# Feed-forward gate tiles in pairs: seven half products in place of eight

## The chip, the cores and the metric

One core of one Trainium2 chip runs the whole program. The metric is the device time of one execution in microseconds (us), the median of several runs. All arithmetic is in fp32; matmuls get their operands as fp32r and the kernel makes fp32 accuracy from them by splitting (below).

## What is computed

The reference is two transformer blocks in a row on 512 tokens of width 1024, with 16 meta tokens ahead of them. Each has two attention branches, a gated mix, and a feed-forward block of width 2816. The change touches the feed-forward blocks only:

```python
hn = rms_norm(h, ffn_norm_g[l])
h = h + (jax.nn.silu(hn @ w_ffn_gate[l]) * (hn @ w_ffn_up[l])) @ w_ffn_down[l]
```

The second block has the same form with its own weights.

## The kernel before

Everything is kept transposed: a tile has 128 features on the partitions and the 512 tokens along the free axis. A product of 128 output features takes one weight tile of 1024 x 128 (eight chunks of 128 x 128, KD = 8) and the eight chunks of the activations. Each operand is split in two fp32r parts, a high part (ScalarE's copy to fp32r) and a low part (the rest, a subtraction by VectorE), and three matmuls stand for one: high x high, high x low, low x high. `product` (L1736) issues them, 24 for a tile, into psL[:, b]; b is 0 or 1 and alternates, so that one half of psL is filled while the other is read.

The weights go through three buffers of two slots each (slot b): `load` (L455, SyncE) brings a tile from HBM into stage[:, b] once the low part of the tile before it in this slot is made (lo[b]); `high` (L720, ScalarE) writes wh[:, b], after the tile has landed (w_in[b]) and TensorE is through with the old wh[:, b] (mm[b]); `low` (L1058, VectorE) writes wl[:, b] and counts lo[b]. TensorE's product waits for lo[b] and for ev[b], the reader's signal that psL[:, b] has been read for the pair before. All of this is counted by a running number of the pair (PAIR0 of the phase, plus i). There is no planner: every engine has its own program, written out by hand, and works through it strictly in order.

The feed-forward block is done in three parts a, b and c of 8, 8 and 6 hidden tiles of 128 (FPARTS, L39). A part has a phase gu, whose pair i is gate tile i (b = 0) and up tile i (b = 1), and a phase dn of four pairs of output tiles. In gu the reader is VectorE's `swiglu` (L1497): gate times R, the tokens' norm factors (L1509); ScalarE's tanh (L936); (tanh + 1) times gate (L1513); up times R (L1515); their product, hid (L1517); ScalarE's high part of hid (L940); VectorE's low part (L1519). ScalarE's side is `swiglu` at L930. In dn, VectorE adds the product to hT (`add_down`, L1531). Before the first gu phase, the out phase makes hn from hT chunk by chunk (`squares_and_gain`, L911: hn at L916, squares at L918), and the first gu pair holds the norm factors' own small matmuls.

GpSimd (POOL) has nothing to do in the feed-forward. TensorE's order there is `layer_rest` at L2028.

Of the kernel before, what the change touches and what calls it, by code (L numbers as in the profile page):

```python
# [29 lines left out]
P = 128  # L30
D = 1024
KD = D // P
SEQ = 512
NB = SEQ // P
# [17 lines left out]

NEAR = 2 * P
# [30 lines left out]
def feed_forward(l):  # L84
    return [f for ab, n in zip("abc", FPARTS) for f in ((f"gu{l}{ab}", 2 * n, KD, 1), (f"dn{l}{ab}", KD, n, 1))]

# [131 lines left out]
def build(nc, t, out):  # L218
    with ExitStack() as ctx:
# [219 lines left out]
        recip_ok, kbm_ok = sem("recip_ok"), sem("kbm_ok")  # L439
        fin_gain, fin_rms, fin_out = sem("fin_gain"), sem("fin_rms"), sem("fin_out")  # L440
# [13 lines left out]
        def _(sp):  # L454
# [38 lines left out]
            def layer_rest(l, win, gates_at, wa, wb, wo, wg, wu, wd):  # L493
# [9 lines left out]
                for part, ab in enumerate("abc"):  # L503
                    f0 = sum(FPARTS[:part])
                    with sp.Fori(0, PAIRS[f"gu{l}{ab}"]) as i:
                        load(f"gu{l}{ab}", i, 0, by_rows(wg), i * P + f0 * P)
                        load(f"gu{l}{ab}", i, 1, by_rows(wu), i * P + f0 * P)
# [206 lines left out]
        def _(act):  # L714
# [196 lines left out]
            def squares_and_gain(name, norm, grow):  # L911

                def chunk(i, b):
# [4 lines left out]
                    act.activation(sq[:], hT[:, bass.ds(2 * i + b, 1), :], ACT.Square).then_inc(h_sq, 1)  # L918

# [10 lines left out]
            def swiglu(name, f0, early=0):  # L930
                def pair(i, last, early=False):
                    high(name, i, 1)
                    if early:
                        high_next(name, i, last)
                    act.wait_ge(ev[0], PAIR0[name] + i + 1)
                    act.activation(ft[:, 1, :], ft[:, 0, :], ACT.Tanh, scale=0.5).then_inc(t_ok, 1)  # L936
                    if not early:
                        high_next(name, i, last)
                    act.wait_ge(hid_ok, f0 + i + 1)
                    act.activation(hid[:, 0, bass.ds(i, 1), :], ft[:, 4, :], ACT.Copy).then_inc(hid_hi, 1)  # L940

                for i in range(early):
                    pair(i, False, True)
                with act.Fori(early, PAIRS[name] - 1) as i:
                    pair(i, False)
                pair(PAIRS[name] - 1, True)
# [3 lines left out]
            swiglu("gu1a", before_part(1, 0), 1)  # L950
            only_high("dn1a")
            swiglu("gu1b", before_part(1, 1))
            only_high("dn1b")
            swiglu("gu1c", before_part(1, 2))
# [65 lines left out]
            swiglu("gu2a", before_part(2, 0), 1)  # L1020
            only_high("dn2a")
            swiglu("gu2b", before_part(2, 1))
            only_high("dn2b")
            swiglu("gu2c", before_part(2, 2))
# [26 lines left out]
        def _(v):  # L1051
# [445 lines left out]
            def swiglu(name, f0, head=None):  # L1497

                def pair(i, last, head=None):
                    low(name, i, 1)  # L1500
                    if head:
                        new_rms(head[0])
                        diagonals(diag, rs[:, 0:4]).then_inc(diag_ok, 1)
                        low_next(name, i, last)
                        v.wait_ge(bcast, head[1])
                        v.tensor_copy(R, psT[:, 1, :]).then_inc(R_ok, 1)
                        v.wait_ge(R_ok, head[1])
                    done(name, i, 0)
                    v.tensor_tensor(ft[:, 0, :], psL[:, 0, :], R, ALU.mult).then_inc(ev[0], 1)  # L1509
                    if not head:  # L1510
                        low_next(name, i, last)
                    v.wait_ge(t_ok, f0 + i + 1)
                    dv.link(v.scalar_tensor_tensor(out=ft[:, 2, :], in0=ft[:, 1, :], scalar=1.0, in1=ft[:, 0, :], op0=ALU.add, op1=ALU.mult))  # L1513
                    done(name, i, 1)
                    v.tensor_tensor(ft[:, 3, :], psL[:, 1, :], R, ALU.mult).then_inc(ev[1], 1)  # L1515
                    v.wait_ge(ev[1], PAIR0[name] + i + 1)
                    v.scalar_tensor_tensor(out=ft[:, 4, :], in0=ft[:, 2, :], scalar=0.5, in1=ft[:, 3, :], op0=ALU.mult, op1=ALU.mult).then_inc(hid_ok, 1)  # L1517
                    v.wait_ge(hid_hi, f0 + i + 1)
                    v.tensor_tensor(hid[:, 1, bass.ds(i, 1), :], ft[:, 4, :], hid[:, 0, bass.ds(i, 1), :].bitcast(F32), ALU.subtract).then_inc(hid_lo, 1)  # L1519

                first = 0
                if head:
                    pair(0, False, head)
                    first = 1
                with v.Fori(first, PAIRS[name] - 1) as i:
                    dv.enter(i - first, 1)
                    pair(i, False)
                dv.leave(PAIRS[name] - 1 - first)
                pair(PAIRS[name] - 1, True)
# [6 lines left out]
            def down(name):  # L1536
                def pair(i, last):
                    low(name, i, 1)
                    add_down(name, i, 0)
                    low_next(name, i, last)  # L1540
                    add_down(name, i, 1)

                pairs(name, pair)
# [3 lines left out]
            swiglu("gu1a", before_part(1, 0), (2, 3))  # L1547
            down("dn1a")
            swiglu("gu1b", before_part(1, 1))
            down("dn1b")  # L1550
            swiglu("gu1c", before_part(1, 2))

# [157 lines left out]
            swiglu("gu2a", before_part(2, 0), (4, 5))  # L1710
            down("dn2a")
            swiglu("gu2b", before_part(2, 1))
            down("dn2b")
            swiglu("gu2c", before_part(2, 2))
# [512 lines left out]
```

## Time and profile before

| | before |
|---|---|
| median of 3 runs | 1549.47 us (1549.3 to 1551.33) |
| the profiled execution's own time | 1552.76 us |
| its span, first to last instruction | 1551.00 us |
| mean granted TensorE clock | 0.995 of full |
| TensorE matmuls | 7356, busy 1521.8 us |
| VectorE busy | 845.6 us |
| ScalarE busy | 532.7 us |
| first feed-forward block, without a wait of TensorE | 411.50 to 735.06 us |

The profile shows one execution. PE is TensorE's matmuls and PEld its weight loads, which run beside them; DVE is VectorE, ACT ScalarE, POOL GpSimd, SP SyncE. Matmuls overlap in the pipeline: a row's duration is longer than the slot that it takes, and the distance between starts tells the pitch. Times in the rows are us from the start of the span unless they are marked ns; [x <-Y] behind a row is the idle time before it and what ended it.

### The profile page before, as it was taken

Reading aid. Unit: us, or ns where it says so; the run is one execution under the profiler, and the core shown is the slowest. Engines: PE = TensorE matmul, PEld = TensorE weight load, DVE = VectorE, ACT = ScalarE, POOL = GpSimd, SP = SyncE. Lnnn points to the kernel's source line nnn. Section 1 sums busy time; section 2 is a strip of 40 time slices with the busy share of each in tenths; the row PEclk is TensorE's granted clock in tenths of the full one; section 3 lists DMA queues with packets and bytes.
Section 4 is the critical chain, followed back from the end, with each engine's and each line's share of the span. In section 5 each row is a group of like instructions: output and inputs, shape, how many; then the busy total and the mean of one; then the engine's idle time right before and its main releaser. Section 6 shows DMA issues by size and latency. Waiting matters only on the chain.

```text
span 1551.0 us, 21003 instructions
## 1 busy us (share of the span) xinstructions
PE 1521.8 (98%) x7356; PEld 1236.4 (80%) x7356; DVE 845.6 (55%) x1520; ACT 532.7 (34%) x929; POOL 242.1 (16%) x206
## 2 busy tenths in 40 slices
PE   7999999999999999999999999999999999999998
PEld 6878886877788888888899777787787888888876
DVE  5578895466555355445854383544655543553454
ACT  5134445533322223222511364444332222221223
POOL 2323334340000000000002563322300000000000
PEclk9999999999999999999999999999999999999999
DMA  6524420033333333332323202121332332333322
GB/s 151 150 55 146 129 55 1 8 92 106 94 95 95 95 95 95 95 94 86 92 84 93 55 2 82 55 61 35 107 96 84 92 103 87 95 95 96 94 81 95
DMA packets 250283, 132.61 MB, mean 85 GB/s; under 512 B 21225, under 2 KB 247653, under 8 KB 250222
## 3 DMA queue, kind: packets, MB, share of 16 engines
q1 hardware_dynamic: 247998, 123.92, 28.1%
q0 software_dynamic: 2144, 7.77, 1.6%
q8 instruction: 35, 0.57, 0.2%
q14 instruction: 26, 0.21, 0.0%
q10 hardware_dynamic: 80, 0.14, 0.0%
HBM read 129.67 MB, written 6.38 MB: 88 GB/s over the span
## 4 chain that ended last, share of the span: by engine, by line
PE 91%; DVE 5%; issue 1%; DMA 1%; ACT 1%; POOL 0%; SPq 0%; DVEq 0%; ACTq 0%; POOLq 0%
PE psL L1756 62%; PE psL L1895 11%; PE psS L1756 5%; PE psT L1904 2%; PE psS L2149 1%; PE psL L2023 1%; PE psS L2172 1%; PE psS L2000 1%; PE psS L1930 1%; PE psL L2126 1%; PE psS L1943 1%; DMA xin<-in_x 1%; PE psS L2105 1%; PE psS L2106 1%; PE psS L1917 0%
## 5 line engine op out<-in xcount | busy, mean ns | idle before, releaser
L1756 PE MATMUL psL<-hn,wh 128*128 128x512 f32 x1680 | 529.0, 396 | 0.2
L1756 PEld LDWEIGHTS psL<-hn,wh 128*128 128x128 f32 x1680 | 314.1, 188 | 76.1 <-issue 1.4
L726 ACT ACTIVATE wh<-stage 128x1024 fp32r<-128x1024 f32 (+3 forms) x250 | 243.3, 973 | 336.4 <-PE psL L1756 243.5
L1756 PE MATMUL psL<-hn,wl 128*128 128x512 f32 x840 | 330.4, 393 | 0.0
L1064 DVE TENSOR_TENSOR wl<-stage,wh 128x1024 fp32r<-128x1024 f32 (+1 forms) x169 | 202.5, 1198 | 93.7 <-ACT wh L726 89.0
L1756 PE MATMUL psL<-hid,wh 128*128 128x512 f32 x704 | 221.5, 395 | 1.3 <-DVE wl L1064 1.3
L576 POOL TENSOR_TENSOR wl<-stage,wh 128x1024 fp32r<-128x1024 f32 (+2 forms) x81 | 154.6, 1909 | 307.3 <-ACT wh L726 307.3
L1756 PEld LDWEIGHTS psL<-hn,wl 128*128 128x128 f32 x840 | 158.0, 188 | 35.8
L1895 PE MATMUL psL<-hn,wh 128*128 128x512 f32 x496 | 173.0, 430 | 0.4 <-DVE yn L1670 0.4
L1756 PEld LDWEIGHTS psL<-hid,wh 128*128 128x128 f32 x704 | 131.3, 187 | 35.3 <-DVE wl L1064 3.0
L1756 PE MATMUL psL<-hid,wl 128*128 128x512 f32 x352 | 138.8, 394 | 0.0
L1895 PEld LDWEIGHTS psL<-hn,wh 128*128 128x128 f32 x496 | 88.7, 189 | 19.3 <-DVE yn L1670 0.8
L940 ACT ACTIVATE hid<-ft 128x512 f32 (+1 forms) x44 | 27.8, 632 | 209.0 <-DVE ft L1517 209.0
L1895 PE MATMUL psL<-hn,wl 128*128 128x512 f32 x248 | 97.9, 395 | 0.0
L1534 DVE TENSOR_TENSOR hT<-hT,psL 128x512 f32 (+1 forms) x48 | 33.0, 688 | 106.0 <-PE psL L1756 106.0
L1756 PE MATMUL psS<-hn,wh 128*128 128x264 f32 x448 | 85.9, 292 | 0.8 <-DVE hn L1114 0.7
L1756 PE MATMUL psL<-mix,wh 128*128 128x512 f32 x256 | 80.7, 396 | 1.0 <-DVE wl L1064 1.0
L936 ACT ACTIVATE ft<-ft 128x512 f32<-128x512 f32 x44 | 27.9, 633 | 149.1 <-DVE ft L1509 149.1
L1756 PEld LDWEIGHTS psL<-hid,wl 128*128 128x128 f32 x352 | 65.9, 187 | 16.2
L1756 PEld LDWEIGHTS psS<-hn,wh 128*128 128x128 f32 x448 | 71.9, 194 | 2.5 <-issue 1.2
L648 POOL MEMSET m8d<- 128x128 f32 x1 | 0.2, 210 | 437.2 <-DVE kaT L1191 437.2
L1756 PE MATMUL psS<-hn,wl 128*128 128x264 f32 x224 | 64.9, 290 | 0.0
(383 smaller groups left out, 1971.4 us busy)
## 6 DMA issues: line engine op xcount, KB each, us to landing
stage<-in_w_in SPq DMA_DIRECT2D x54, 512.0 KB, 3.9
stage<-in_w_ffn_gate SPq DMA_DIRECT2D x22, 512.0 KB, 3.8
stage<-in_w_ffn_up SPq DMA_DIRECT2D x22, 512.0 KB, 3.8
stage<-in_w_ff_gate SPq DMA_DIRECT2D x22, 512.0 KB, 3.8
stage<-in_w_ff_up SPq DMA_DIRECT2D x22, 512.0 KB, 3.8
stage<-in_w_out SPq DMA_DIRECT2D x16, 512.0 KB, 3.8
stage<-in_w_ffn_down SPq DMA_DIRECT2D x16, 512.0 KB, 3.8
stage<-in_w_ff_down SPq DMA_DIRECT2D x16, 512.0 KB, 3.9
```

The lines of the kernel that those rows point to most:

```text
L576: pool.tensor_tensor(wl[:, b, 0:n], stage[:, b, 0:n], wh[:, b, 0:n].bitcast(F32), ALU.subtract).then_inc(lo[b], 1)
L726: act.activation(wh[:, b, 0:n], stage[:, b, 0:n], ACT.Copy).then_inc(hi[b], 1)
L936: act.activation(ft[:, 1, :], ft[:, 0, :], ACT.Tanh, scale=0.5).then_inc(t_ok, 1)
L940: act.activation(hid[:, 0, bass.ds(i, 1), :], ft[:, 4, :], ACT.Copy).then_inc(hid_hi, 1)
L1064: v.tensor_tensor(wl[:, b, 0:n], stage[:, b, 0:n], wh[:, b, 0:n].bitcast(F32), ALU.subtract).then_inc(lo[b], 1)
L1534: v.tensor_tensor(hT[:, n, :], hT[:, n, :], psL[:, b, :], ALU.add).then_inc(ev[b], 1)
L1756: ins = pe.matmul(dst, w[:, b, k * P:(k + 1) * P], x[:, part, k, c0:c1], start=k + n == 0, stop=k == kc - 1 and n == 2)
L1895: ins = pe.matmul(psL[:, b, :], w[:, b, k * P:(k + 1) * P], hn[:, part_, k, META:], start=k + n == 0, stop=k == KD - 1 and n == 2)
L1904: ins = pe.transpose(psT[:, n % 2, m * P:(m + 1) * P], tile[:, col:col + P], ident[:])
L1930: pe.matmul(psS[:, 2 * (j % 2), 0:W], aqT[:, h % 4, i * P:(i + 1) * P], akz[:, h // 4, k0:k0 + W], start=True, stop=True).then_inc(p["s"], 1)
L1943: ins = pe.matmul(psS[:, 2 * (i % 2) + 1, h * HD:(h + 1) * HD], PTa[:, u % 2, n * P:(n + 1) * P], avn[:, c, h // 4 * HD:h // 4 * HD + HD], ...
L2000: ins = pe.matmul(psS[:, 2 * (j % 2) + bank, 0:k1 - k0], q, kz[:, h, k0:k1], start=True, stop=True)
```

## The change

A gate tile's product is written as a 2 x 2 block product: two gate tiles (rows i and i + 1) by the two halves of the contraction (chunks 0 to 3, 4 to 7), times two halves of the tokens (256 each). In place of eight products of blocks come seven, by Strassen's scheme in the form with shared sums; each is 4 chunks x 3 split matmuls of 256 columns. Up tiles, down tiles and the first four gate tiles of part a are made as before. For this, the change

- loads two gate tiles as one pair and then the two up tiles as the next pair;
- makes a copy hg of the activations with their gain (ScalarE, in the out phase) and, in pairs 1 to 3 of part a, four sums of token blocks from it, each 128 x 1024, with high and low parts (xt);
- makes for each gate pair four sums of weight blocks (VectorE, 128 x 512 each), with high (ScalarE) and low (VectorE) parts, two of 128 x 1024 each;
- takes interim results out of PSUM by ScalarE (part_x, part_z) and adds them on VectorE.

```diff
+GATE_PLAIN = (4, 0, 0)
...
 # SyncE, layer_rest
+                    for i in range(GATE_PLAIN[part]):
+                        load(f"gu{l}{ab}", i, 0, by_rows(wg), (f0 + i) * P)
+                        load(f"gu{l}{ab}", i, 1, by_rows(wu), (f0 + i) * P)
+                    for i, _ in gate_pairs(l, part):
+                        for b in range(2):
+                            load(f"gu{l}{ab}", i, b, by_rows(wg), (f0 + i + b) * P)
+                        for b in range(2):
+                            load(f"gu{l}{ab}", i + 1, b, by_rows(wu), (f0 + i + b) * P)
...
 # ScalarE, squares_and_gain
+                    act.activation(hg[:, bass.ds(2 * i + b, 1), :], hT[:, bass.ds(2 * i + b, 1), :], ACT.Copy,
+                                   scale=gvec[:, bass.ds(2 * i + (grow + b), 1)]).then_inc(hg_ok, 1)
 # ScalarE
+            def sum_high(pair, half):
+                act.wait_ge(ws_sum, 2 * pair + half + 1)
...
+                act.activation(wsh[:, cols], wsum[:, cols], ACT.Copy).then_inc(ws_hi, 1)
+            def second_high(name, i):
+                act.wait_ge(w_in[1], 16 * (LOAD0[name] + LOADS[name]) + i * (16 * LOADS[name]))
+                act.wait_ge(mm[1], PAIR0[name] + i)
+                act.activation(wh[:, 1, SEQ:2 * SEQ], stage[:, 1, SEQ:2 * SEQ], ACT.Copy).then_inc(hi[1], 1)
...
+            def swiglu(l, part):
...
+                for i in range(plain):
                     high(name, i, 1)
+                    if i == 0:
+                        high_next(name, i, False)
                     act.wait_ge(ev[0], PAIR0[name] + i + 1)
                     act.activation(ft[:, 1, :], ft[:, 0, :], ACT.Tanh, scale=0.5).then_inc(t_ok, 1)
+                    if i:
+                        high_next(name, i, False)
+                    if i == 1:
+                        token_sum_high(l, 0)
+                        token_sum_high(l, 1)
+                        inner_high(i, f0)
+                        token_sum_high(l, 2)
+                    elif i == 2:
+                        token_sum_high(l, 3)
+                        inner_high(i, f0)
+                    elif i == plain - 1:
+                        sum_high(pairs_[0][1], 0)
+                        inner_high(i, f0)
+                        sum_high(pairs_[0][1], 1)
...
+                second_high(name, pairs_[0][0])
+                for i, n in pairs_:
+                    last = i == pairs_[-1][0]
+                    act.wait_ge(acc_x, 3 * n + 1)
+                    act.activation(part_x[:, 0:HT], psS[:, 0, 0:HT], ACT.Copy).then_inc(out_x, 1)
+                    high(name, i + 1, 0)
+                    act.wait_ge(mm[1], PAIR0[name] + i + 1)
+                    act.activation(part_z[:, 0:HT], psS[:, 3, 0:HT], ACT.Copy).then_inc(out_z, 1)
+                    high(name, i + 1, 1)
+                    act.wait_ge(acc_y, 2 * n + 1)
+                    act.activation(part_z[:, HT:], psS[:, 2, 0:HT], ACT.Copy).then_inc(out_y, 1)
+                    act.wait_ge(acc_x, 3 * n + 2)
+                    act.activation(part_x[:, HT:], psS[:, 0, 0:HT], ACT.Copy).then_inc(out_x, 1)
...
+                    if not last:
+                        sum_high(n + 1, 0)
+                    high_next(name, i + 1, last)
+                    inner_high(i, f0)
+                    if not last:
+                        sum_high(n + 1, 1)
+                        second_high(name, i + 2)
+                    inner_high(i + 1, f0)
...
 # VectorE, swiglu: the plain pairs of part a
                     done(name, i, 0)
                     v.tensor_tensor(ft[:, 0, :], psL[:, 0, :], R, ALU.mult).then_inc(ev[0], 1)
+                    if i == first - 1:
+                        weight_sums(name, first, pair0)
+                    if i:
+                        low_next(name, i, False)
+                    opened(i, f0, ft[:, 0, :], ft[:, 1, :])
+                    if i == 1:
+                        token_sum(l, 0)
+                        token_sum(l, 1)
+                        token_sum_low(l, 0)
+                        token_sum(l, 2)
+                    elif i == 2:
+                        token_sum_low(l, 1)
+                        token_sum(l, 3)
+                        token_sum_low(l, 2)
+                    elif i == first - 1:
+                        sum_low(pair0, 0)
+                    times_up(name, i, 1, i, f0, ft[:, 0, :])
+                    if i == first - 1:
+                        second_low(name, first)
+                    inner_low(i, f0)
+                    if i == first - 1:
+                        sum_low(pair0, 1)
 # VectorE, swiglu: a gate pair and its up pair
+                for i, n in pairs_:
+                    last = i == pairs_[-1][0]
+                    done(name, i, 0)
+                    v.wait_ge(out_x, 2 * n + 1)
+                    v.tensor_tensor(ft[:, 0, 0:HT], psS[:, 1, 0:HT], part_x[:, 0:HT], ALU.add).then_inc(ev[0], 1)
+                    low(name, i + 1, 0)
+                    low(name, i + 1, 1)
+                    v.wait_ge(acc_y, 2 * n + 2)
+                    v.wait_ge(out_x, 2 * n + 2)
+                    dv.link(v.tensor_tensor(ft[:, 0, HT:], psS[:, 2, 0:HT], part_x[:, HT:], ALU.add))
+                    v.tensor_tensor(ft[:, 0, :], ft[:, 0, :], R, ALU.mult).then_inc(gate_ok, 1)
...
+                    opened(i, f0, ft[:, 0, :], ft[:, 1, :])
+                    opened(i + 1, f0, ft[:, 2, :], tanh2[:])
+                    if not last:
+                        weight_sums(name, i + 2, n + 1)
+                    times_up(name, i, 0, i + 1, f0, ft[:, 0, :])
+                    low_next(name, i + 1, last)
+                    if not last:
+                        sum_low(n + 1, 0)
+                    inner_low(i, f0)
+                    if not last:
+                        sum_low(n + 1, 1)
+                    times_up(name, i + 1, 1, i + 1, f0, ft[:, 2, :])
+                    if not last:
+                        second_low(name, i + 2)
+                    inner_low(i + 1, f0)
...
 # TensorE
+            def half_product(dst, weights, c0, x, add=False):
+                whi, wlo = weights
+                for k in range(KD // 2):
+                    cols = slice(c0 + k * P, c0 + (k + 1) * P)
+                    for n, (w, part) in enumerate(((whi, 0), (whi, 1), (wlo, 0))):
+                        ins = pe.matmul(dst, w[:, cols], x(part, k), start=not add and k + n == 0, stop=k == KD // 2 - 1 and n == 2, skip_group_check=True)
+                return ins
+            def gate_pair(name, i, n, l):
...
+                for b in range(2):
+                    pe.wait_ge(ev[b], PAIR0[name] + i)
+                pe.wait_ge(lo[0], PAIR0[name] + i + 1)
+                half_product(x, first, 0, rows_of(0, 0)).then_inc(acc_x, 1)
+                half_product(psS[:, 1, 0:HT], first, SEQ, rows_of(KD // 2, 0)).then_inc(mm[0], 1)
+                pe.wait_ge(lo[1], PAIR0[name] + i + 1)
+                pe.wait_ge(xt_lo, 4 * l)
+                half_product(z, second, SEQ, token_sums(3)).then_inc(mm[1], 1)
+                pe.wait_ge(ws_lo, 2 * n + 1)
+                half_product(y, mixed, 0, token_sums(0)).then_inc(acc_y, 1)
+                pe.wait_ge(out_x, 2 * n + 1)
+                half_product(x, mixed, SEQ, token_sums(1), add=True).then_inc(acc_x, 1)
+                pe.wait_ge(ws_lo, 2 * n + 2)
+                pe.wait_ge(out_y, n + 1)
+                half_product(y, mixed, 2 * SEQ, rows_of(KD // 2, HT), add=True).then_inc(acc_y, 1)
+                pe.wait_ge(out_x, 2 * n + 2)
+                half_product(x, mixed, 3 * SEQ, token_sums(2), add=True).then_inc(acc_x, 1)
+                for b in range(2):
+                    product(name, i + 1, b, hn)
```

`weight_sums` waits for both of the gate pair's loads and issues four tensor_tensor of 128 x 512; `sum_low` is one subtraction of 128 x 1024 after its `sum_high`; `second_low` one of 128 x 512 after `second_high`; `token_sum` and `token_sum_low` are one of 128 x 1024 each. `times_up` is up times R, which counts ev[b], and then hid; `opened` is (tanh + 1) times gate; `inner_low` is the low part of hid. In `down` the weight sums, the sum_low and the second_low for the next part's first gate pair stand in the last pair.

## Rows read from the trace of the kernel before

**Rows 1.** The page: busy time by engine, TensorE's clock in slices, chain's shares
```profile
PE 1521.8 (98%) x7356; PEld 1236.4 (80%) x7356; DVE 845.6 (55%) x1520; ACT 532.7 (34%) x929; POOL 242.1 (16%) x206
...
PEclk9999999999999999999999999999999999999999
...
PE 91%; DVE 5%; issue 1%; DMA 1%; ACT 1%; POOL 0%; SPq 0%; DVEq 0%; ACTq 0%; POOLq 0%
PE psL L1756 62%; PE psL L1895 11%; PE psS L1756 5%; PE psT L1904 2%; PE psS L2149 1%; PE psL L2023 1%; PE psS L2172 1%; PE psS L2000 1%; PE psS L1930 1%; PE psL L2126 1%; PE psS L1943 1%; DMA xin<-in_x 1%; PE psS L2105 1%; PE psS L2106 1%; PE psS L1917 0%
```

**Rows 2.** The chain in order of time (start, us, what): the two feed-forward blocks
```profile
411.50 323.56 PE psL L1756 x1392
...
1179.52 323.57 PE psL L1756 x1392
```

**Rows 3.** Busy time of each engine in two stretches of the feed-forward
```profile
core 0: us, PE busy (x) PEld busy (x) DVE busy (x) ACT busy (x) POOL busy (x), PEclk, DMA share, GB/s
...
600.00:700.00 100.00, 100.00 (x432) 80.67 (x431) 44.09 (x51) 24.30 (x28) 0.00 (x0) 1.00 0.32 95
1210.00:1310.00 100.00, 100.00 (x432) 80.67 (x431) 44.41 (x51) 23.91 (x29) 0.00 (x0) 1.00 0.32 95
```

**Rows 4.** VectorE's timeline over one pair of part a (start, us, engine, instruction)
```profile
428.64 0.69 DVE L1509 TENSOR_TENSOR ft<-psL,Rk 128x512 f32<-128x512 f32 x1 [1.10 <-PE psL L1756]
430.98 1.22 DVE L1064 TENSOR_TENSOR wl<-stage,wh 128x1024 fp32r<-128x1024 f32 x1 [1.65 <-ACT wh L726]
432.12 0.68 DVE L1513 SCALAR_TENSOR_TENSOR ft<-ft 128x512 f32<-128x512 f32 x1
434.27 0.69 DVE L1515 TENSOR_TENSOR ft<-psL,Rk 128x512 f32<-128x512 f32 x1 [1.47 <-PE psL L1756]
...
439.76 0.69 DVE L1509 TENSOR_TENSOR ft<-psL,Rk 128x512 f32<-128x512 f32 x1 [1.11 <-PE psL L1756]
```

**Rows 5.** The chain in order of time: the stretch of matmuls with 264 columns
```profile
783.33 49.07 PE psS L1756 x405
```

**Rows 6.** VectorE's groups by form: 1024, 768 and 512 elements (busy us, mean ns)
```profile
L1064 DVE TENSOR_TENSOR wl<-stage,wh 128x1024 fp32r<-128x1024 f32 x153 | 187.3, 1224 | 85.9 <-ACT wh L726 81.2
...
L1515 DVE TENSOR_TENSOR ft<-psL,Rk 128x512 f32<-128x512 f32 x44 | 30.4, 692 | 62.8 <-PE psL L1756 62.7
...
L1064 DVE TENSOR_TENSOR wl<-stage,wh 128x768 fp32r<-128x768 f32 x16 | 15.2, 950 | 7.8 <-ACT wh L726 7.8
```

**Rows 7.** ScalarE's groups by form: 1024, 512 and 256 elements
```profile
L726 ACT ACTIVATE wh<-stage 128x1024 fp32r<-128x1024 f32 x198 | 208.2, 1052 | 295.9 <-PE psL L1756 203.0 <-PE psS L1756 68.7 <-PE psL L1895 22.7
...
L940 ACT ACTIVATE hid<-ft 128x512 f32 x36 | 22.7, 632 | 175.5 <-DVE ft L1517 175.5
...
L852 ACT ACTIVATE PTa<-psT 128x256 f32<-128x256 f32 x32 | 11.9, 373 | 8.9 <-PE psT L1904 8.9
```

**Rows 8.** DMA issues: KB each, median us from issue to landing
```profile
stage<-in_w_ffn_gate SPq DMA_DIRECT2D x22, 512.0 KB, 3.8
```

**Rows 9.** TensorE's timeline where a gate product ends
```profile
438.87 0.62 PE L1756 MATMUL psL<-hn,wh 128*128 128x512 f32 x2
439.33 0.39 PE L1756 MATMUL psL<-hn,wl 128*128 128x512 f32 x1
```

**Rows 10.** VectorE's and then TensorE's timeline where TensorE waited for a read
```profile
410.75 0.69 DVE L1509 TENSOR_TENSOR ft<-psL,Rk 128x512 f32<-128x512 f32 x1
...
411.50 0.74 PE L1756 MATMUL psL<-hn,wh 128*128 128x512 f32 x2
412.08 0.40 PE L1756 MATMUL psL<-hn,wl 128*128 128x512 f32 x1
```

**Rows 11.** ScalarE's groups by form: the gain copy of the out phase
```profile
L916 ACT ACTIVATE hn<-hT,gvec x12 | 8.7, 724 | 42.2 <-DVE hT L1477 42.2
```

**Rows 12.** Busy time in stretches near the start; the clock stands before the DMA share
```profile
22.00:24.00 2.00, 1.25 (x9) 0.82 (x7) 1.97 (x7) 1.43 (x3) 0.00 (x0) 1.00 0.00 0
24.00:28.00 4.00, 4.00 (x21) 4.00 (x22) 3.43 (x13) 3.16 (x6) 0.00 (x0) 0.57 0.42 108
28.00:30.00 2.00, 2.00 (x19) 2.00 (x18) 1.78 (x10) 0.91 (x1) 0.00 (x0) 1.00 0.86 314
```

More of the change, by code:

```diff
@@ L33 @@
 SEQ = 512
+HT = SEQ // 2
 NB = SEQ // P
@@ L85, in feed_forward, with gate_pairs_before, gate_pairs @@
     return [f for ab, n in zip("abc", FPARTS) for f in ((f"gu{l}{ab}", 2 * n, KD, 1), (f"dn{l}{ab}", KD, n, 1))]
+GATE_PLAIN = (4, 0, 0)
+assert all((n - m) % 2 == 0 for n, m in zip(FPARTS, GATE_PLAIN))
+def gate_pairs_before(l, part):
+    counts = [(n - m) // 2 for n, m in zip(FPARTS, GATE_PLAIN)]
+    return (l - 1) * sum(counts) + sum(counts[:part])
+def gate_pairs(l, part):
+    first = gate_pairs_before(l, part)
+    return [(p, first + (p - GATE_PLAIN[part]) // 2) for p in range(GATE_PLAIN[part], FPARTS[part], 2)]
 def before_part(l, part):
@@ L940, in pair @@
[L940 to L946, printed above, removed]
+                    if i:
[12 more added lines that the diff above has]
+                        sum_high(pairs_[0][1], 1)
+                    else:
+                        inner_high(i, f0)
@@ L1500, in pair, with inner_low, swiglu @@
+            def inner_low(i, f0):
+                v.wait_ge(hid_hi, f0 + i + 1)
+                v.tensor_tensor(hid[:, 1, i, :], ft[:, 4, :], hid[:, 0, i, :].bitcast(F32), ALU.subtract).then_inc(hid_lo, 1)
+            def swiglu(l, part, head=None):
+                name, f0, pairs_ = f"gu{l}{'abc'[part]}", before_part(l, part), gate_pairs(l, part)
+                first, pair0 = pairs_[0]
+                for i in range(first):
                     low(name, i, 1)
-                    if head:
+                    if i == 0:
@@ L1507, in pair @@
                         v.wait_ge(R_ok, head[1])
+                    if i == first - 1:
+                        token_sum_low(l, 3)
                     done(name, i, 0)
                     v.tensor_tensor(ft[:, 0, :], psL[:, 0, :], R, ALU.mult).then_inc(ev[0], 1)
[L1510 to L1513, printed above, removed]
@@ L1521, in swiglu @@
[L1521 to L1529, printed above, removed]
+                    if i == first - 1:
+                        weight_sums(name, first, pair0)
+                    if i:
+                        low_next(name, i, False)
@@ L1539, in pair @@
                     add_down(name, i, 0)
+                    if last:
+                        weight_sums(nxt, first, pair0)
                     low_next(name, i, last)
+                    if last:
+                        sum_low(pair0, 0)
                     add_down(name, i, 1)
+                    if last:
+                        second_low(nxt, first)
+                        sum_low(pair0, 1)
                 pairs(name, pair)
@@ L2051, in layer_rest @@
                 product(name, 0, 1, hn, between={(0, 1): norm_sums, (0, 6): norm_spread})
-                products(name, hn, first=1)
-                products(f"dn{l}a", hid, made=(hid_lo, before_part(l, 0)))
-                for part, ab in enumerate("bc", 1):
-                    products(f"gu{l}{ab}", hn)
+                for i in range(1, GATE_PLAIN[0]):
+                    for b in range(2):
+                        product(name, i, b, hn)
+                for part, ab in enumerate("abc"):
+                    for i, n in gate_pairs(l, part):
+                        gate_pair(f"gu{l}{ab}", i, n, l)
                     products(f"dn{l}{ab}", hid, made=(hid_lo, before_part(l, part)))
```

146 lines of the change are left out of this document (111 added, 35 removed).

## The prediction

> **What bounds the kernel now.** I read the shares and the clock on the page first [rows 1]: TensorE's row is at 98% of the span, VectorE's at 55%, ScalarE's at 34%, and TensorE's granted clock is full in all forty slices. The chain that ended last is TensorE for 91%, 62% of it at L1756, the split products. A busy matmul row is not yet a bound, so the next view is the chain itself [rows 2]: each feed-forward block is one unbroken piece, 323.56 and 323.57 us long, in which no matmul waited for anything. The stretches inside it [rows 3] add that VectorE has 44 us of work in 100, ScalarE 24, POOL none, DMA a third. So in the feed-forward TensorE's own pitch is the bound, everything else has slack, and both can change: matmul columns taken out shorten the span one for one, and any wait that TensorE now gets lengthens it by its full length.
>
> **What the change takes away.** One pair of today (gate and up tile) takes 11.12 us: VectorE's read of the gate tile starts at 428.64 and the next at 439.76 [rows 4]. It is 48 matmuls, so one of 512 columns costs 231.7 ns. The change makes two gate tiles (48 matmuls, 11.12 us) from seven half products of 12 matmuls with 256 columns: 84. No row has 256 columns in this form; the nearest is 264, and 405 of those took 49.07 us [rows 5], 121.2 ns each. The line through (512, 231.7) and (264, 121.2) gives 117.6 ns at 256. I take that: 84 × 117.6 = 9.88 us, a gain of 1.24 per gate pair. The ends are half of the 512 price (115.9: gain 1.39) and the full 264 price (121.2: gain 0.94). Part a keeps four plain pairs, so a layer has 2 + 4 + 3 = 9 gate pairs: 9 × 1.24 = **11.2 us** per layer saved (8.5 to 12.5).
>
> The Trainium skill (TensorE: Matmul & The Clock Gate, Back-to-back issue gap) states N/2.4 + 2.5 ns for a stream at full clock, 109.2 ns for 256 columns and 215.8 for 512. This trace disagrees at 512 (231.7) and at 264 (121.2 against 112.5), so the rows decide; with 109.2 for the half products alone the gain would be 1.95 per pair and the whole sum below would be 12.8 us lower, still not a gain.
>
> **What the change adds: waits of TensorE.** I priced the new instructions by their nearest rows and followed the three queues in program order. VectorE: 1024 elements 1.22 us, 512 elements 0.69, 256 elements 0.42 (0.27 per 256 elements less than 512) [rows 6]; ScalarE: 1.05 for 1024, 0.63 for 512, 0.37 for 256 out of PSUM [rows 7]. An instruction that depends on the one before starts 0.04 after it; an independent one starts some 0.09 before the other's end (432.12 against 430.98 + 1.22 [rows 4]). A weight load from HBM is 3.8 us from issue to landing [rows 8]. A product is ready for VectorE 0.20 us after its last slot (last wl matmul at 439.33 with a slot of 0.23, reader at 439.76 [rows 9, 4]). A stopped TensorE starts 0.06 after the release (411.44 to 411.50) and its first slots come 0.12 late (wh, wh to wl takes 0.58 us instead of 0.46 [rows 10, 9]); I take 0.16 in all.
>
> (1) **The hand-over before each gate pair.** gate_pair waits for ev[b] of the pair before, for both b. ev[1] is VectorE's read of psL[:, 1], the product that TensorE has only just finished. In the old order the other half of psL covered this read; now nothing does: 0.20 + 0.69 + 0.16 = 1.05 us with TensorE stopped. It comes before 8 gate pairs per layer (the ninth is in (2)): **8.4 us**. The condition is that VectorE stands ready. After the sixth half product (time 0) its queue is: add2 0.20, times R 0.67, z add at 1.61, times R 2.34, two openings 3.07 and 3.80, four weight sums from 4.53, the up tile's read at 7.20, hid 7.93, next low 8.54, sum_low 9.68, inner_low 10.82, sum_low 11.42 to 12.65. psL[:, 1] is ready at 1.41 + 11.12 + 0.20 = 12.73. So VectorE is just in time, by about 0.1 us; in the last pair of a part it has less to do, and the down phase hands over with room.
>
> (2) **The start of part a**, where four token sums, their low halves and the first weight sums stand in the queues of plain pairs 1 to 3. Time 0 is VectorE's read of gate tile 1. It runs: read 0.69, low(2, 0) until 3.59, opening until 4.19, then token_sum 0, 1, token_low 0, token_sum 2 (four of 1.22 + 0.04) until 9.26, and only then the read of up tile 1 and hid, until 10.71. ScalarE's inner_high(1) waits for that hid, and queued behind it are token_sum_high 2 and high(2, 1), which ends at 13.31; low(2, 1) ends at 14.58 and TensorE goes on at 14.74. It was free at 11.12: 3.62 us. Once more a pair later (token_low 1, token_sum 3, token_low 2 ahead of hid, then inner_high and high(3, 1)): 1.14. In pair 3 VectorE does token_low 3, waits for gate tile 5's weights (issued after low(3, 1), landing at 30.7), makes four sums, low(4, 0), the opening and sum_low until 36.4, and only then reads psL[:, 1]: TensorE goes on at 37.24 and was free at 32.57: 4.68. Inside this first gate pair second_low comes late (its ScalarE half stands behind sum_high): 0.82 before the third half product. The load it releases lands 3.8 us later, ScalarE's high(5, 1) waits for it, and behind high stands the copy of y that the sixth half product needs: 0.98. Together **11.2 us** per layer. In later gate pairs the same copy is ready 0.6 us before it is wanted.
>
> Costed at nothing: the gained copy hg (8 × 0.72 us on ScalarE in the out phase, where it idles 42.2 / 12 = 3.5 us ahead of each L916 [rows 11]; if that cover were gone, 5.8 us per layer); copies of x, y, z (under other half products); the tail into the down phase, whose last hidden tile is wanted 24 × 0.23 - 0.70 = 4.9 us after its start and comes at 3.0; DMA, as bytes and loads stay the same.
>
> **Sum per layer**: -11.2 + 8.4 + 11.2 = +8.5 (unrounded); two layers: **+17 us**. Made against the profiled execution of 1552.76 us (its span is 1551.00), which lies 3.3 us over the median of the three timed runs, 1549.47. A difference carries over to either: 1549.5 + 17 = **1566.5 us**. About 3 us (0.2%) is what a measurement of this kernel can tell from no change.
>
> **Rivals.**
> - **VectorE becomes the bound between gate pairs.** It is at the reader's place with 0.1 us to spare in the 6 transitions per layer inside a part. If the strided or broadcast forms cost 0.5 us more per pair, all of it lands on TensorE: 12 × 0.5 = 6 us, 1572.5. Against it: POOL is silent [rows 3], and today's operations there keep 0.69 and 1.22 to 0.01 us [rows 4]. Chance 0.16.
> - **The clock falls in the 4.7 us stop.** After the broken start of the kernel, the granted clock was 0.57 over 24 to 28 us and 1.00 behind it [rows 12]: level 1.2 GHz for a while, worth 4 × 0.43 = 1.7 us. No stop near 4.7 us in a warm block is in this trace, so the chance is open. Twice: +3.4, 1570. Chance 0.14. The Trainium skill (same page, The HAM clock gate) also says that idle gaps throttle the array again; the sum without it stands on the rows.
> - **The other side: part a's pile-up dissolves.** If (2) does not bite, because low(2, 1) is there within the 5.56 us of one product (ScalarE not held by inner_high behind the token sums), 22.4 us go and the sum is +17 - 22.4 = -5.4: 1544, faster. It decides at lo[1] of pair 2 against 11.12 on the clock above, and I have it 3.5 us late, by rows good to 0.05. Chance 0.05.
> - **It does not save what it says**: half products at the 264 price save 17.0 instead of 22.4; +22.3, 1572. Chance 0.10. At 115.9 instead the sum is +14.3, inside my case.
> - **A break-even mix**: part (2) half as large and 115.9 ns, +3: 1552.5. Chance 0.05.
>
> **How the numbers follow.** The forecast has 0.50. The range must hold 8 in 10: from 1559 (pitch 115.9 and a quarter off the stops of part a) to 1577 (VectorE late and the clock fallen on top). Slower by over 0.2%: 0.50 + 0.16 + 0.14 + 0.10 and part of the mix = 0.92; within 0.2%: 0.04; faster: 0.04.
>
> **What would show it.** Right: rows with psS of 128x256 at a pitch near 118 ns; 16 stops of about 1.05 us ahead of gate pairs released by the times-R read of psL; per layer one stop near 3.6 and one near 4.7 us in part a, released by low and by that read; VectorE near 80% busy. Wrong: no idle of TensorE before gate pairs, stops well over 1.05 released by sum_low or weight sums (VectorE bound), a feed-forward piece shorter than 323.6 us, or 256-column matmuls away from 116 to 121 ns.

## The result, and the profile after

The changed kernel takes 1570.57 us (median of 4 runs, 1569.77 to 1574.27) against 1550.4 us for the kernel before (4 runs): ratio 1.0134, 95% interval 1.0115 to 1.0153. It is slower by 20 us; forecast were 17 (1566.5, range 1559 to 1577).

The page of the changed kernel, the lines that answer to [rows 1]:

```profile
PE 1511.6 (96%) x8004; PEld 1256.9 (80%) x8004; DVE 969.5 (62%) x1698; ACT 612.6 (39%) x1061; POOL 242.1 (15%) x206
...
PEclk9999999999989999999999999999999999999999
...
PE 86%; DVE 7%; issue 3%; ACT 2%; DMA 2%; SPq 0%; POOL 0%; DVEq 0%; ACTq 0%; POOLq 0%
```

TensorE is busy 10 us less and the span is longer; on the chain its share fell from 91% to 86%, and VectorE, ScalarE, DMA and "issue" took the rest. The clock's row, full in all forty slices before, has one slice below 9. The chain in order of time says where. The first feed-forward block was one row of 323.56 us [rows 2]; now it is this (start, us, what):

```profile
411.21 5.83 PE psL L1970 x24
...
421.27 1.24 DVE ta L1607
...
425.05 1.24 DVE ta L1607
426.31 0.70 DVE ft L1651
...
428.30 1.04 ACT xt L989
429.34 0.95 ACT wh L766
430.32 1.23 DVE wl L1167
...
443.75 3.81 DMA stage<-in_w_ffn_gate
...
447.65 0.70 DVE wsum L1624
...
454.10 12.62 PE psS L1993 x84
466.72 11.14 PE psL L1970 x48
477.86 0.83 issue
478.69 10.22 PE psS L1993 x84
488.91 55.94 PE psL L1970 x240
...
567.16 0.83 issue
567.99 10.24 PE psS L1993 x84
578.23 11.14 PE psL L1970 x48
589.37 0.95 issue
590.33 10.19 PE psS L1993 x84
...
734.07 11.15 PE psL L1970 x48
```

The block runs from 411.21 to 734.07 + 11.15 = 745.22: 334.0 us, 10.4 more. The second one, from 1186.73 to 1519.90, takes 333.2, 9.6 more. Together that is the 20 us. (The spans of the two profiled executions, 1551.0 and 1567.8, differ by less: before's execution had a clock of 0.94 over 885 to 932 us in the second block's attention, worth 3 us, and the same work took 44 us in place of 47 in the other one. Differences of this size between executions stand in every comparison below.)

Two things are to be seen. Ahead of each later group of 84 matmuls (seven half products of 12) stands a stop of 0.83 to 0.99 us. The profile calls it "issue": it names no releaser for it. The times below point to VectorE's read, and the first and the last experiment test that. And part a is a ladder of VectorE, ScalarE and a load until 454. VectorE at two of these stops, by the timeline (start and duration in us, engine, line, operation):

```profile
565.84 1.22 DVE L1636 TENSOR_TENSOR wsl<-wsum,wsh 128x1024 fp32r<-128x1024 f32 x1
567.20 0.69 DVE L1651 TENSOR_TENSOR ft<-psL,Rk 128x512 f32<-128x512 f32 x1
...
588.40 1.22 DVE L1636 TENSOR_TENSOR wsl<-wsum,wsh 128x1024 fp32r<-128x1024 f32 x1
589.54 0.68 DVE L1651 TENSOR_TENSOR ft<-psL,Rk 128x512 f32<-128x512 f32 x1
```

TensorE at the second of them, by its timeline:

```profile
588.97 0.40 PE L1970 MATMUL psL<-hn,wl 128*128 128x512 f32 x1
590.33 0.47 PE L1993 MATMUL psS<-hn,wh 128*128 128x256 f32 x2 [0.95 <-issue]
```

The last product ends at 589.37, the read of its result ends at 590.22, and the half products begin 0.11 later. They write psS, not psL; they wait all the same. At the first stop (0.83) VectorE was through with sum_low at 567.06, 0.10 before the product's end at 567.16. At the second (0.95) it was still busy until 589.62, because its second opening had waited 0.40 us for ScalarE's tanh: here the read began 0.17 us behind the product's end, at the first 0.04. So VectorE is close to the edge here.

### The profile page after: what moved, and what is told of

It is laid out like the page before. It is cut to its first block, busy times and chain, and to the rows that moved or that the text cites. A ratio compares the mean times of both kernels' runs of the same rounds, so it can differ in the third digit from the quotient of the medians.

```text
span 1567.8 us, 21882 instructions
## 1 busy us (share of the span) xinstructions
PE 1511.6 (96%) x8004; PEld 1256.9 (80%) x8004; DVE 969.5 (62%) x1698; ACT 612.6 (39%) x1061; POOL 242.1 (15%) x206
## 4 chain that ended last, share of the span: by engine, by line
PE 86%; DVE 7%; issue 3%; ACT 2%; DMA 2%; SPq 0%; POOL 0%; DVEq 0%; ACTq 0%; POOLq 0%
PE psL L1970 46%; PE psS L1993 12%; PE psL L2149 11%; PE psS L1970 5%; PE psT L2158 2%; PE psS L2405 1%; PE psL L2277 1%; PE psS L2428 1%; PE psS L2254 1%; PE psS L2184 1%; PE psS L2197 1%; PE psL L2382 1%; DMA xin<-in_x 1%; PE psS L2361 1%; DVE wl L1167 1%
## 5 line engine op out<-in xcount | busy, mean ns | idle before, releaser
L766 ACT ACTIVATE wh<-stage 128x1024 fp32r<-128x1024 f32 (+3 forms) x232 | 225.4, 971 | 368.4 <-PE psL L1970 248.5
L1970 PE MATMUL psL<-hn,wh 128*128 128x512 f32 x1104 | 352.5, 401 | 7.1 <-DVE wl L1167 6.7
L1970 PEld LDWEIGHTS psL<-hn,wh 128*128 128x128 f32 x1104 | 206.5, 190 | 57.0 <-DVE wl L1167 8.1
L1970 PE MATMUL psL<-hn,wl 128*128 128x512 f32 x552 | 218.9, 397 | 0.0
L1167 DVE TENSOR_TENSOR wl<-stage,wh 128x1024 fp32r<-128x1024 f32 (+1 forms) x151 | 180.3, 1194 | 61.4 <-ACT wh L766 61.2
L2149 PE MATMUL psL<-hn,wh 128*128 128x512 f32 x496 | 173.0, 430 | 0.4 <-DVE yn L1884 0.4
L1970 PEld LDWEIGHTS psL<-hn,wl 128*128 128x128 f32 x552 | 104.9, 190 | 24.2
L2149 PEld LDWEIGHTS psL<-hn,wh 128*128 128x128 f32 x496 | 88.7, 189 | 19.3 <-DVE yn L1884 0.8
L2149 PE MATMUL psL<-hn,wl 128*128 128x512 f32 x248 | 98.0, 395 | 0.0
L1993 PE MATMUL psS<-xt,wsh 128*128 128x256 f32 x432 | 79.2, 283 | 0.0
L1993 PE MATMUL psS<-hn,wh 128*128 128x256 f32 x288 | 57.5, 300 | 21.5 <-issue 13.6
L1970 PEld LDWEIGHTS psS<-hn,wh 128*128 128x128 f32 x448 | 71.6, 193 | 2.2 <-issue 1.2
L1993 PEld LDWEIGHTS psS<-hn,wh 128*128 128x128 f32 x288 | 47.7, 203 | 28.9 <-issue 28.9
```

What stands on the lines that cost most here:

```text
L766: act.activation(wh[:, b, 0:n], stage[:, b, 0:n], ACT.Copy).then_inc(hi[b], 1)
L1167: v.tensor_tensor(wl[:, b, 0:n], stage[:, b, 0:n], wh[:, b, 0:n].bitcast(F32), ALU.subtract).then_inc(lo[b], 1)
L1970: ins = pe.matmul(dst, w[:, b, k * P:(k + 1) * P], x[:, part, k, c0:c1], start=k + n == 0, stop=k == kc - 1 and n == 2)
L1993: ins = pe.matmul(dst, w[:, cols], x(part, k), start=not add and k + n == 0, stop=k == KD // 2 - 1 and n == 2, skip_group_check=True)
L2149: ins = pe.matmul(psL[:, b, :], w[:, b, k * P:(k + 1) * P], hn[:, part_, k, META:], start=k + n == 0, stop=k == KD - 1 and n == 2)
```

## Experiments

The account on trial: half products save what they should (theory 1, the price), but TensorE stands still at each hand-over (theory 2) and in part a, where token sums lengthen the queues (theory 3), with a slower clock behind the long stops (theory 4). The rivals are a VectorE that is the bound, and half products that cost more than 118 ns. The edits are shown against the changed kernel unless something else is said, with "..." where lines are left out.

### The hand-over wait taken out

```diff
-                for b in range(2):
-                    pe.wait_ge(ev[b], PAIR0[name] + i)
                 pe.wait_ge(lo[0], PAIR0[name] + i + 1)
                 half_product(x, first, 0, rows_of(0, 0)).then_inc(acc_x, 1)
```

> The changed kernel without gate_pair's wait for ev[b] (its half products write psS only; the read of psL that ev[1] reports is waited for again by the up products behind them). Hand-over theory: the 16 stops of about 1 us ahead of gate pairs go, but the next wait stands 0.5 us behind: the copy of y waits behind ScalarE's high of the up tile, whose load starts only after second_low, so the sixth half product stops 0.4 us in the 6 transitions per layer inside a part; and the stops at the start of part a keep their sum (less ahead of the pair, more before its third half product). Some 6 us less per layer: 1570.6 - 12 = 1558.5 us. Rival, VectorE is the bound: TensorE stops as long elsewhere (for sum_low or low), and the time stays within 3 us of 1570.6. Rival, the price of the half products is the loss: same stops gone, but gate pairs' 84 matmuls take longer than 10.1 us.

Measured: 1563.5 us, ratio to before 1.009 (1.0072 to 1.0108). 7 us came back, not 12. A cycle of gate pair and up pair takes 21.76 us ((595.19 - 551.67) / 2 below) where it took 22.2; without any stop it would be 21.04 (next experiment). So the stops of 1.2 us went and one of 0.7 us stands in their place. The chain of this kernel shows it:

```profile
551.67 11.15 PE psL L1970 x48
564.89 3.95 DMA stage<-in_w_ffn_up
570.33 3.06 PE psS L1993 x24
...
586.73 3.91 DMA stage<-in_w_ffn_up
592.13 3.05 PE psS L1993 x24
595.19 11.15 PE psL L1970 x48
```

Only 24 of the 84 half products' matmuls are behind the wait: the sixth and the seventh. They wait for the copy of y, which in ScalarE's queue stands behind its high of the second up tile, which waits for the load:

```profile
590.66 1.06 ACT L766 ACTIVATE wh<-stage 128x1024 fp32r<-128x1024 f32 x1 [1.56 <-DMA stage<-in_w_ffn_up]
591.62 0.36 ACT L1035 ACTIVATE part_z<-psS 128x256 f32<-128x256 f32 x1
```

I had this stop as 0.4 us in 6 transitions per layer; it is 0.7, and it stands in nearly all of them.

### The copy of y ahead of the load

Against the kernel of the last section:

```diff
-                    high(name, i + 1, 1)
                     act.wait_ge(acc_y, 2 * n + 1)
                     act.activation(part_z[:, HT:], psS[:, 2, 0:HT], ACT.Copy).then_inc(out_y, 1)
+                    high(name, i + 1, 1)
```

> As e1, and ScalarE copies y out of PSUM before its high of the second up tile instead of behind it. Hand-over theory: the 0.4 us stop ahead of the sixth half product goes too (14 of them or so with the 0.9 us one of part a's first pair): 3.3 us less per layer than e1, 1558.5 - 6.6 = 1552 us, and outside part a TensorE has no stop at all. VectorE-bound rival: no difference to e1.

Measured: 1555.6 us, ratio 1.0028 (1.0008 to 1.0047), 8 us less than the last one and 15 less than the change (1552 was expected). Behind part a's stops the chain of both blocks has nothing but TensorE:

```profile
555.29 11.13 PE psL L1970 x48
566.43 9.90 PE psS L1993 x84
576.33 11.13 PE psL L1970 x48
587.47 9.90 PE psS L1993 x84
```

Two readings follow. The price: 84 matmuls in 9.90 us are 117.9 ns each, against my 117.6 (theory 1 holds, its rival falls). And the cycle without a wait is 587.47 - 566.43 = 21.04 us, so a hand-over in the changed kernel, whose cycles inside a part take 22.16 to 22.29 us, costs 1.12 to 1.25 us. VectorE does the same work in a cycle of 21.04 us as in one of 22.2, so its load is not what sets the cycle.

### 256 columns by themselves

Against the kernel before, for 42 of its 44 gate products:

```diff
+                if name[:2] == "gu" and b == 0 and made is None:
+                    parts = [(psL[:, b, 0:SEQ // 2], META, META + SEQ // 2), (psL[:, b, SEQ // 2:SEQ], META + SEQ // 2, NKEY)]
...
```

> The kernel before, with 42 of its 44 gate products made as two halves of 256 columns each (48 matmuls in place of 24, same order of chunks, same psL bank, no scheme, no sums). It prices 256 columns by themselves. At 118 ns a matmul, as in the runs without stops: 48 x 0.118 - 5.56 = +0.10 us per product, 42 of them, +4 us: 1554.7. Rival, 121 ns or more (the price of the 264-column rows): +10 us, 1561.

Measured: 1553.89 us beside 1551.83 for the kernel before, ratio 1.0011 (0.9999 to 1.0024). That is 2 us where 4 were expected, and by the time alone 118 ns can hardly be told from no cost; the chain is finer:

```profile
412.76 325.19 PE psL L1758 x1896
```

325.19 - 323.56 [rows 2] is 1.63 us for 21 products: 0.078 each, and with 24 x 0.2317 = 5.56 us for a product before, (5.56 + 0.078) / 48 = 117.5 ns. At the 264-column price of 121.2 the block would have been 5.4 us longer.

### One more operation in VectorE's queue

```diff
                         sum_low(n + 1, 1)
+                        v.tensor_tensor(tmp[:, 0, :], R, R, ALU.add)
                     times_up(name, i + 1, 1, i + 1, f0, ft[:, 2, :])
```

> The changed kernel with one more VectorE addition of 128x512 (0.60 us, result unused) ahead of the read of the second up tile, in the 6 transitions per layer inside a part. My account has VectorE there with 0.1 to 0.2 us to spare, so 0.4 to 0.5 us of each lands on TensorE: 12 x 0.45 = +5.5 us, 1576. Rival, VectorE has room (its 62% busy share): no change, 1570.6. Rival, VectorE was already late: the full 0.6 each, +7.

Measured: 1574.09 us, ratio 1.0143 (1.0112 to 1.0174), whose interval overlaps the changed kernel's. The cycle is the better reading:

```profile
558.14 11.14 PE psL L1971 x48
570.49 10.20 PE psS L1994 x84
580.68 11.14 PE psL L1971 x48
```

The stop is 1.21 us (570.49 less the product's end at 569.28) where 0.83 stood, and the same 1.20 to 1.21 stand ahead of the other gate pairs of the first block that have the extra operation; the cycle is 22.54 us. So 0.38 of the added 0.60 us reaches TensorE, close to the 0.4 to 0.5 expected: VectorE had some 0.2 us to spare. That it has room by its 62% falls, and so does that it was late everywhere already.

### Part a's queues spread out, the wait kept

```diff
-GATE_PLAIN = (4, 0, 0)
+GATE_PLAIN = (6, 0, 0)
...
 # ScalarE, plain pairs
                     act.activation(ft[:, 1, :], ft[:, 0, :], ACT.Tanh, scale=0.5).then_inc(t_ok, 1)
+                    if 1 <= i < 5:
+                        token_sum_high(l, i - 1)
...
+                    if i == plain - 1:
+                        sum_high(pairs_[0][1], 0)
+                        second_high(name, pairs_[0][0])
+                    inner_high(i, f0)
...
 # VectorE, plain pairs: behind the gate tile's read
+                    if i == 1:
+                        token_sum(l, 0)
+                    elif 2 <= i < 5:
+                        token_sum_low(l, i - 2)
...
 # and behind inner_low
+                    if 1 <= i < 4:
+                        token_sum(l, i)
+                    elif i == 4:
+                        token_sum_low(l, 3)
+                    elif i == first - 1:
+                        sum_low(pair0, 0)
+                        sum_low(pair0, 1)
```

> The changed kernel with its hand-over wait kept, but six plain gate pairs in part a instead of four, with at most one token sum or low half ahead of each read and second_high ahead of inner_high. One gate pair less per layer (1.05 us of gain lost, one 1.0 us hand-over saved). Queue theory: the stops of 3.6 and 4.7 us in part a shrink to one of 3.6 us ahead of the first gate pair (four weight sums ahead of low and of the read), 7.5 us less per layer: 1570.6 - 15 = 1555.5 us. If the long stops also cost clock, up to 2 us more comes back, and the granted clock stays at 1.00 in part a unless the 3.6 us stop drops it. Rival, the token sums are harmless: 1570 us.

Measured: 1561.35 us, ratio 1.0068 (1.0051 to 1.0084): 9 us less than the change, 15 were expected. The first block runs from 412.97 to 740.24, 327.3 us, 6.7 less than the changed kernel's; the second some 5 less, as two of its later gate pairs met a second stop behind loads that took 5.1 and 4.7 us. (The rest of the profiled execution outside the two blocks was 4 us longer than the changed kernel's, which is the spread between executions.) The stop of 3.6 us in pair 2 is gone; the one ahead of the first gate pair is 3.60, as expected. What took back part of the gain is behind it, in the chain:

```profile
472.56 11.66 PE psS L1983 x84
```

and in the windows over the same stretch (start:end and length; busy us of TensorE, its weight loads, VectorE, ScalarE and GpSimd, with counts; the granted clock, the DMA engines' share and GB/s):

```profile
472.00:474.00 2.00, 1.44 (x7) 1.47 (x8) 1.87 (x4) 0.78 (x2) 0.00 (x0) 0.60 0.81 241
474.00:476.00 2.00, 2.00 (x12) 2.00 (x12) 2.00 (x3) 1.18 (x2) 0.00 (x0) 0.55 0.49 141
```

The 84 took 11.66 us in place of 10.19, where the granted clock is 0.60 and 0.55: 1.5 us in the first block and 1.4 in the second.

### All three

No wait, copy of y first, queues spread with six plain pairs.

> All three together: no wait for ev[b], copy of y first, six plain pairs with spread token sums. Both theories of TensorE's stops together: one stop near 2.2 us and one of 0.3 us per layer are left; 8 gate pairs save 8 x (11.12 - 10.10) = 8.2 us per layer. Time per layer 5.7 us under the kernel before: 1550.4 - 11.3 = 1539 us, faster than both. If the scheme itself were the loss (price of half products, VectorE's load): 1550 us or more.

Measured: 1541.91 us, ratio 0.994 (0.9921 to 0.9959), faster than the kernel before. 1539 were expected. The remaining stop of part a is 2.40 us in the first block, and even behind that one the clock fell. The chain:

```profile
471.25 11.78 PE psS L1983 x84
```

The windows, in the columns of the last ones:

```profile
471.00:473.00 2.00, 1.75 (x12) 1.75 (x13) 1.93 (x4) 0.00 (x0) 0.00 (x0) 0.81 0.15 42
473.00:475.00 2.00, 2.00 (x11) 2.00 (x11) 1.91 (x4) 1.72 (x3) 0.00 (x0) 0.50 0.74 223
...
1232.00:1234.00 2.00, 2.00 (x18) 2.00 (x18) 1.93 (x4) 0.19 (x1) 0.00 (x0) 1.00 0.43 125
```

The last line is the same place in the second block of the same execution. There the stop was 2.26 us, the clock stayed at 1.00, and the 84 took 10.58 us (1231.77 to 1242.35, with a short wait for sum_low in it) in place of 11.78.

### The stop filled with spare matmuls

Against the kernel of the last section:

```diff
+                if i == 6 and name[3] == "a":
+                    for _ in range(9):
+                        pe.matmul(psT[:, 0, :], hn[:, 0, 0, META:META + P], hn[:, 0, 0, META:NKEY], start=True, stop=True)
                 pe.wait_ge(lo[0], PAIR0[name] + i + 1)
```

> e6_best with nine spare matmuls of 512 columns (9 x 0.232 = 2.1 us, into a bank of psT that nobody reads here) in the 2.4 us stop ahead of part a's gate pair. They add no work for any other engine. Clock theory: behind that stop e6_best ran at the 1.2 GHz level for some 3 us, its 84 half products took 11.8 us in place of 9.9; with TensorE kept busy the granted clock stays at 1.00 and the 84 take 10.2: 1.5 us per layer, 1541.9 - 3 = 1539 us. Rival, the long 84 come from waits and not from the clock: 11.8 us again, 1542.

Measured: 1537.88 us, ratio 0.9918 (0.9899 to 0.9938), 4 us less than the kernel without them; the intervals of the two ratios overlap, so the time alone does not decide. In the first block the half products begin at 470.37 and end at 480.60, 10.23 us in place of 11.78, at full clock. The chain:

```profile
470.37 4.22 PE psS L1983 x36
474.61 5.99 PE psS L1983 x48
```

The windows, with a granted clock of 1.00 where 0.50 stood:

```profile
472.00:474.00 2.00, 2.00 (x20) 2.00 (x19) 1.90 (x4) 1.94 (x4) 0.00 (x0) 1.00 0.63 183
474.00:476.00 2.00, 1.98 (x17) 1.78 (x16) 2.00 (x4) 1.13 (x2) 0.00 (x0) 1.00 0.84 237
```

In the second block, where the clock had not fallen without them either, they bring nothing: 10.58 us (1228.96 to 1239.54) in both kernels. So the long 84 go with the granted clock and not with a wait (theory 4). That filling a stop keeps the clock up is shown by one pair of stretches only.

### Part a plain, seven half products in parts b and c only

As in "All three", but GATE_PLAIN = (8, 0, 0): the token sums stay spread over part a, and the plain pairs lose their weight sums, since the last pair of the down phase makes them for part b.

> As e6_best, but all eight gate tiles of part a are plain and the seven half products are used in parts b and c only: 7 gate pairs per layer, the first behind a down phase, whose last pair holds the weight sums without a stop. No stop of TensorE is left in the feed-forward. 7 x (11.12 - 9.91) = 8.5 us per layer, 17 in all: 1550.5 - 17 = 1533.5 us, faster than e6_best by 8. If the token sums or the scheme cost something that the stops do not show: slower than e6_best.

Measured: 1537.74 us, ratio 0.9912 (0.9892 to 0.9933), and in a second set 1536.25 (ratio 0.9893, 0.9872 to 0.9914). That is 4 us less than with six plain pairs, where 8 were expected (the runs of that kernel spread from 1536.12 to 1544.82), and the same as with six plain pairs and the filled stop (1537.88). Its first block takes 315.8 us (411.36 to 727.14), 7.8 less than before; 7 x 1.23 would be 8.6. With seven gate pairs per layer it is 33 us faster than the change with nine: no stop of part a stands ahead of any of them, and none has the hand-over.

### The hand-over by itself

The last kernel with gate_pair's wait put back, and nothing else.

> e7_part_a_plain with gate_pair's wait for ev[b] put back, and nothing else. There are 7 gate pairs per layer and no other stop, so this is the hand-over alone: 14 x 1.17 us (the changed kernel's period of 22.2 us against 21.04 without the wait) = +16 us on 1537.7, so 1554 us, about the time of the kernel before. My prediction's price of 1.05 would give +14.7, 1552.5. Rival, the stops only hide other waits (as the missing wait of e1 uncovered the one for the copy of y): +8 us or less.

> e7_part_a_plain once more, beside e9_wait_back on the same chip, for their difference: 1537.7 us by its first run.

Measured beside each other: 1552.39 and 1536.25 us, ratios to before 1.0000 (0.9986 to 1.0014) and 0.9893. The difference of 16.1 us over 14 gate pairs is 1.15 us each, beside 1.17 expected; that the stops only hide other waits is excluded (+8 us or less). One wait, which protects nothing here, costs nearly as much as the seven half products bring (1.23). The chain of the kernel with the wait shows it:

```profile
547.94 11.14 PE psL L1948 x48
559.08 0.83 issue
559.90 10.19 PE psS L1971 x84
```

Two of its 14 stops are longer, 1.42 and 1.52 us; at both VectorE was still at sum_low when the product was ready.

## Why the prediction was right

**What bounds it.** TensorE alone, with everything else in slack: right. What lies between the two kernels in the feed-forward is a slot of TensorE, a stop of it, or its clock.

**The gain.** 117.6 ns per half product's matmul, 1.24 us per pair. Measured 117.9 in the stream and 117.5 by themselves: 11.13 - 9.90 = 1.23. The line through 512 and 264 columns was right to 0.3 ns. The half products are not all alike: see below.

**(1), the hand-over.** Place, number (8 per layer, 16 in all) and releaser were right; the size was a little small, 1.05 against 1.12 to 1.25 in the profile and 1.15 by the experiment. The sum's term is 9.4 us in the first block and 8.9 in the second instead of 8.4. The restart after it was the part I took low: 1.12 - 0.20 - 0.69 leaves 0.23 us where 0.16 stood, and the half products begin 0.10 to 0.11 us after the read's end, where 0.06 stood in [rows 10]. "VectorE stands ready" held with about the room I gave it: it was through with sum_low 0.10 us before the product's end, and by the extra operation it had some 0.2 us to spare. Where the tanh came late, or at the end of a down phase, it was late itself (stops of 0.95 and 0.99). So that rival was near, and at these two stops it cost 0.12 and 0.16 us.

**(2), part a.** The chain came as worked out: four token operations of 1.26 us, the read, hid, token_sum_high 2, high, low (421.27 to 431.55). TensorE went on at 431.60, 14.53 us after the gate tile's read at 417.07, where I had 14.74. The first stop was priced 3.62 and the weight loads sat idle 3.80 us before it; the third was priced 4.68 and they sat idle 4.39. The stops of 1.14, 0.82 and 0.98 us did not appear. In their place the clock fell behind both long stops: it was 0.83 over 430 to 440 us, worth 1.7 us, and 0.54 over 454 to 460, where the 84 matmuls took 12.62 us in place of 9.90, worth 2.7. TensorE was slower there, so what it would have waited for came in time. An example: by an estimate from 117.9 ns, two half products at full clock would have ended near 457.0, and the low part that the third one needs was ready at 457.57; at the slow clock the third began at 459.35.

So the rival **the clock falls** came true, in each block behind two stops and not only behind the one of 4.7 us, and it cost more than the 1.7 us per layer I gave it; but it took the place of the small stops rather than standing on top of them. Part a costs 10.4 + 9 x 1.23 - 9.4 = 12.1 us in the first block and 9.6 + 9 x 1.23 - 8.9 = 11.8 in the second, against 11.2. In the first block that is 4.4 us of clock and 7.7 for the two long stops, priced 8.3. That the term came out so near is in part luck: 2.9 us of small stops were not there, and the 4.4 us of clock were not in the sum. The rival's chance of 0.14 was too low. I took a 4.7 us stop as the open case; in a later kernel the clock fell behind one of 2.40 us too.

**The sum.** -11.1 + 9.4 + 12.1 = +10.4 in the first block and -11.1 + 8.9 + 11.8 = +9.6 in the second, where +8.5 stood: 20 us in place of 17. Half of the rest is the hand-over and half is part a.

**The price by the Trainium skill.** The half products' 117.9 ns against 109.2 says that the formula that the prediction takes from the Trainium skill (TensorE: Matmul & The Clock Gate, Back-to-back issue gap) is not the price of this form, at 256 columns as at 512. (That page of the Trainium skill has these figures for matmuls back to back, but the section named calls the formula that of an isolated one.)

**What was costed at nothing** (hg, the copies, the down phase's tail, the bytes) stayed at nothing, as far as the chain shows, but for one: the copy of y was "ready 0.6 us before it is wanted" only because the hand-over had TensorE waiting. Without it the copy holds TensorE up by 0.7 us. A slack that is read off a timeline with a stop in it holds only as long as the stop.

## What to carry to other kernels

A stream of dense work on one engine is paid for in slots, and a scheme that saves a tenth of them is nearly lost to one full hand-over per group: look at each wait of the bound engine for whether it protects the buffer that is written next, and give the groups buffers of their own that wait for their own readers only. When a stop goes, expect the next one close behind it and follow the queues again. One-off preparation costs least where the bound engine's queue has cover left. A part that needs it at its very start may as well be left as it was: with all of part a plain the kernel took 1537.74 us, and with its last two gate tiles in the scheme and the stop filled 1537.88.

## What the runs showed that I had not expected

The granted clock falls behind stops that look harmless. In a block that had run dense for 56 us, a stop of 2.40 us was followed by a stretch at 0.50, the 1.2 GHz level (some 1.5 us lost). Over the profiled executions of all these kernels, every stop of the weight loads of 3.1 us or more in these blocks was followed by that level, and so was one of 2.32 us in the first kernel without the wait. Stops of 2.26, 2.00 and 1.88 us were not, and the hand-overs, 1.2 to 1.9 us by the weight loads, never were. With the stop of 2.40 us filled with spare matmuls the same half products ran at 2.4 GHz throughout; but the kernel without them kept its clock in its other block, so that the filling did it is not shown beyond this one stretch.

Half products of one shape differ in pitch by their operands. In the stream without stops, three matmuls take 0.351 us with hn and wh, 0.340 with xt and wh, 0.360 with xt and wsh (from the starts of low parts at 566.50 and 568.96, 569.30 and 570.32, 570.67 and 573.19, in the kernel with the copy of y first). No run here tells what in the operands it is, and I leave it open.
